# A two-layer diffusion backbone with mixture-of-experts layers: tokens turned inside the gate/up passes, bf16 slot tables, a two-pair weight ring

## The reference

```python
scores = sigmoid(t @ router_w)
sel = scores + router_bias             # 4 of 8 groups, then the top 8 experts of a token
w = take(scores, idx); w = w / sum(w) * ROUTED_SCALE
...                                    # the tokens of each expert, in blocks
yb = (silu(t[tok] @ w_gate[e]) * (t[tok] @ w_up[e])) @ w_down[e] * w_b
routed = zeros.at[tok].add(yb);  out = routed + swiglu(t, shared weights)
```

## Time and profile before

| | |
|---|---|
| median of 3 runs | 2326.23 us (2323.54 to 2328.62) |
| profiled execution | 2326.45 us, its span 2324.6 us |
| TensorE busy | 1915.4 us (82% of the span) |
| VectorE / ScalarE / GpSimd busy | 1145.3 / 794.1 / 318.6 us |
| moved by DMA | 597.07 MB, mean 257 GB/s |
| first expert stage | about 467 to 1208 us |
| second expert stage | about 1702 to 2279 us |

### The profile page before, as it was taken

How to read it: one execution, slowest core, us unless ns; L and a number is a source line. 1 busy time by engine, 2 the same in 40 slices (tenths; PEclk the granted TensorE clock), 3 DMA queues, 4 the chain that set the end, 5 groups by cost and what they waited for, 6 DMA issues and landing times. The chain is left out here.

```text
span 2324.6 us, 33561 instructions
## 1 busy us (share of the span) xinstructions
PE 1915.4 (82%) x9971; PEld 1298.1 (56%) x9972; DVE 1145.3 (49%) x2242; ACT 794.1 (34%) x1292; POOL 318.6 (14%) x333
## 2 busy tenths in 40 slices
PE   2889897899999999999974987637778788878783
PEld 0778744467777777777741971103445555555551
DVE  2325622577777777777748565893131121212114
ACT  1214411155555555555521557870101111111110
POOL 0220010111111211211210101221001111111110
PEclk8999987899999999999987997768889999999997
DMA  6850055068998899999955416304439999999994
GB/s 239 296 188 1 1 224 202 9 251 323 339 339 330 327 342 345 348 333 343 330 191 220 137 55 194 109 18 128 185 144 418 414 392 388 400 411 402 418 366 173
DMA packets 139045, 597.07 MB, mean 257 GB/s; under 512 B 32632, under 2 KB 51128, under 8 KB 79728
## 3 DMA queue, kind: packets, MB, share of 16 engines
q1 hardware_dynamic: 103264, 509.97, 58.3%
q0 software_dynamic: 35584, 84.31, 9.7%
q10 hardware_dynamic: 144, 2.10, 0.2%
HBM read 596.17 MB, written 56.20 MB: 281 GB/s over the span
## 5 line engine op out<-in xcount | busy, mean ns | idle before, releaser
L1459 DVE TENSOR_TENSOR m_w_lo<-m_wgu,m_w_hi 128x1024 fp32r<-128x1024 f32 x264 | 312.6, 1221 | 170.6 <-ACT m_w_hi L1383 157.1
L1383 ACT ACTIVATE m_w_hi<-m_wgu 128x1024 fp32r<-128x1024 f32 x264 | 266.9, 1051 | 205.6 <-DMA m_wgu<-in_moe_w_up 153.0
L1630 PE MATMUL ps<-m_wgu,m_xT 128*64 128x256 f32 x2112 | 261.4, 403 | 78.9 <-DMA m_wgu<-in_moe_w_up 60.1
L1630 PEld LDWEIGHTS ps<-m_wgu,m_xT 128*64 128x64 f32 x2112 | 185.7, 145 | 165.8 <-issue 122.5
L1325 PE MATMUL ps<-m_wd,m_hidT 128*128 128x512 f32 x528 | 237.6, 593 | 0.3 <-ACT m_hidT L1407 0.3
L1340 PE MATMUL ps<-m_w_hi,m_x_hi 128*128 128x512 f32 x528 | 212.8, 403 | 7.2 <-DVE m_x_lo L1451 6.5
L1340 PE MATMUL ps<-m_w_lo,m_x_hi 128*128 128x512 f32 x528 | 208.1, 394 | 0.0
L1340 PE MATMUL ps<-m_w_hi,m_x_lo 128*128 128x512 f32 x528 | 207.2, 392 | 0.0
L1725 DVE SCALAR_TENSOR_TENSOR m_hid<-m_act_g,m_meta,ps 128x256 f32<-128x256 f32 x33 | 15.9, 480 | 337.9 <-ACT m_act_g L1679 337.9
L1325 PEld LDWEIGHTS ps<-m_wd,m_hidT 128*128 128x128 f32 x528 | 95.3, 190 | 95.1 <-issue 95.1
L1266 POOL DMA_INDIRECT y_rows<-h,m_sidx x66 | 67.5, 1023 | 554.5 <-DVE h L1467 554.5
(11 more groups left out here) (316 smaller groups left out, 3429.9 us busy)
## 6 DMA issues: line engine op xcount, KB each, us to landing
m_wgu<-in_moe_w_gate SPq DMA_DIRECT2D x132, 1024.0 KB
m_wgu<-in_moe_w_up SPq DMA_DIRECT2D x132, 1024.0 KB
m_wd<-in_moe_w_down SPq DMA_DIRECT2D x132, 1024.0 KB, 9.9
c_rows<-y_rows SPq DMA_DIRECT2D x12, 2048.0 KB, 15.9
mods<-in_ada_w POOLq DMA_DIRECT2D x11, 1024.0 KB, 6.3
mods<-in_ada_w SPq DMA_DIRECT2D x11, 1024.0 KB, 4.8
mods<-in_lru_w_in SPq DMA_DIRECT2D x7, 1280.0 KB, 6.9
ada_w<-in_ada_w SPq DMA_DIRECT2D x8, 1024.0 KB, 17.5
```

The lines of the kernel that those rows point to most:

```text
L1383: act.activation(w_hi[:, :, k, :], wgu[:, q, :, k, :], ACT.Copy).then_inc(hi_s, 1)
L1459: dve.tensor_tensor(w_lo[:, :, k, :], wgu[:, q, :, k, :], w_hi[:, :, k, :].bitcast(F32), ALU.subtract).then_inc(lo_s, 1)
L1630: last = pe.matmul(g.ps[half[s], GU, a * FE:(a + 1) * FE], xT[:, k, half[s]], wgu[:, s, a, k, :], start=(k == 0), stop=(k == KD - 1))
```

## The change

- First stage, TensorE: `turn_tokens` of the next block stands behind chunk 1 of gate/up (`TURN_AT = 1`) instead of behind chunk 3. ScalarE and VectorE take `tokens` behind their chunk 1, and chunk 2 after it.
- Both stages: `routes.entry` and the one-hot matrices are bf16. Each of the three numbers is stored as three bf16 pieces that add up to it, so the product has 9 columns instead of 3, and VectorE adds the pieces (`tensor_reduce`), then makes the row index from the sum, with a wait between. `pick` is one `scalar_tensor_tensor` for all tiles (one for each block of the pair in the second stage) instead of one `tensor_scalar` for each tile. `route_phase` fills the pieces: some constant fills ahead of the scores, and two subtractions and three copies behind them; a chain of small instructions for each tile goes.
- Second stage: `wgu` holds two pairs, with semaphores for each. `prefetch` issues both pairs (10 MB instead of 6). In the loop the weights of gate and up are loaded two pairs ahead, those of down one pair ahead as before. The loops are unrolled by two; 33 pairs remain.

```diff
-        self.entry = sb(n + "entry", [P, tiles, EXPERTS, 3])
+        self.entry = sb(n + "entry", [P, tiles, EXPERTS, 3 * PIECES], BF16)
...
-        self.wgu = sb(tag + "wgu", [P, 2, 2, KD, FE])
+        self.wgu = sb(tag + "wgu", [P, 2, 2, 2, KD, FE])
...
     def prefetch(self, sp):
...
+        for q in range(2):
+            for s in range(2):
+                self.gate(sp, 2 * q + s, q, s)
+            for s in range(2):
+                self.up(sp, 2 * q + s, q, s)
+            if q == 0:
+                for s in range(2):
+                    self.down(sp, s, s)
...
+                chain.link(dve.tensor_tensor(weight[:], weight[:], wsum[:, :, None].to_broadcast([P, tiles, E]), ALU.mult))
+                for m in range(PIECES):
+                    piece = routes.entry[:, :, :, GAIN * PIECES + m]
+                    chain.link(dve.tensor_copy(piece, weight[:]))
+                    if m + 1 < PIECES:
+                        chain.link(dve.tensor_tensor(weight[:], weight[:], piece, ALU.subtract))
...
-        onehot = sb("onehot", [P, 2, tiles, S])
+        onehot = sb("onehot", [P, 2, tiles, S], BF16)
...
-                        last = pe.matmul(g.ps[0:S, MB + q, 0:3], onehot[:, q, t, :],
+                        last = pe.matmul(g.ps[0:S, MB + q, 0:3 * PIECES], onehot[:, q, t, :],
...
                         last.then_inc(chunk_used, 1)
-                    turn_tokens(i + q, 1 - q)
+                        if c == TURN_AT:
+                            turn_tokens(i + q, 1 - q)
...
                     if split:
-                        split_high(i + q, 1 - q, range(CHUNKS - 1))
+                        split_high(i + q, 1 - q, range(TURN_AT + 1))
+                    tokens(i + q, 1 - q)
+                    if split:
+                        split_high(i + q, 1 - q, range(TURN_AT + 1, CHUNKS - 1))
                     act.wait_ge(chunk_used, CHUNKS * (b + 1))
...
                         split_high(i + q, 1 - q, range(CHUNKS - 1, CHUNKS))
-                    tokens(i + q, 1 - q)
...
-                    for t in range(tiles):
-                        last = dve.tensor_scalar(onehot[:, q, t, :], g.field("iota")[:, 0:S], routes.slot[:, t, bass.ds(e, 1)],
-                                                 g.table[:, bass.ds(b + FIELD[f"negbase{layer}"][0], 1)], ALU.subtract, ALU.is_equal)
-                    last.then_inc(onehot_s, 1)
+                    dve.scalar_tensor_tensor(onehot[:, q, :, :], routes.slot[:, :, bass.ds(e, 1)].to_broadcast([P, tiles, S]),
...
-                    dve.tensor_copy(meta[:, bass.ds(b, 1), :].rearrange("p o c -> p (o c)"), g.ps[0:S, MB + q, 0:3]).then_inc(meta_v, 1)
-                    dve.tensor_scalar(gidx[q][:], g.ps[0:S, MB + q, 0:1], FAR, None, ALU.add).then_inc(idx_s, 1)
+                    pieces = g.ps[0:S, MB + q, 0:3 * PIECES]
+                    dve.tensor_reduce(meta[:, bass.ds(b, 1), :].rearrange("p o c -> p (o c)"), pieces.rearrange("p (c m) -> p c m", m=PIECES),
+                                      AX.X, ALU.add).then_inc(meta_v, 1)
+                    dve.wait_ge(meta_v, b + 1)
+                    dve.tensor_scalar(gidx[q][:], meta[:, bass.ds(b, 1), 0], FAR, None, ALU.add).then_inc(idx_s, 1)
...
+                def gate_up(before, q):
+                    i = before + 1
...
+                    sp.wait_ge(gate_done, before)
                     sp.sem_inc(issue, 1)
                     for s in range(2):
-                        weights.gate(sp, experts[s], s)
-                    sp.wait_ge(up_done, i)
+                        weights.gate(sp, experts[s], q, s)
+                    sp.wait_ge(up_done, before)
...
+                turns = rounds_after_first(sp)
+                with sp.Fori(0, turns) as m:
+                    gate_up(2 * m + 1, 0)
+                    down(2 * m + 1)
+                    gate_up(2 * m + 2, 1)
+                    down(2 * m + 2)
+                gate_up(2 * turns + 1, 0)
+                down(2 * turns + 1)
+                down(2 * turns + 2)
```

More of the change, by code:

```diff
@@ L70 @@
 FAR = 8192.0
+PIECES = 3
+DEST, GAIN = 1, 2
 def slots_of(tiles):
@@ L930, in prefetch @@
     def prefetch(self, sp):
-        for s in range(2):
-            self.gate(sp, s, s)
-        for s in range(2):
-            self.up(sp, s, s)
-        for s in range(2):
-            self.down(sp, s, s)
+        for q in range(2):
[6 more added lines that the diff above has]
+                    self.down(sp, s, s)
 def route_phase(g, layer, tiles, routes, weights):
@@ L1087, in shared_out @@
                     dve.tensor_tensor(g.x[:, t, :], g.x[:, t, :], gated, ALU.add).then_inc(xadd, 1)
+                tok0 = g.field("tok")[:, 0:1, None].to_broadcast([P, tiles, E])
+                for t in range(tiles):
+                    chain.done(dve.memset(routes.entry[:, t, :, 0], t * P - FAR))
+                    chain.done(dve.memset(routes.entry[:, t, :, DEST * PIECES], TOPK * t * P - FAR))
+                chain.done(dve.memset(routes.entry[:, :, :, 2], 0.0))
+                chain.done(dve.tensor_copy(routes.entry[:, :, :, 1], tok0))
+                chain.done(dve.tensor_scalar(routes.entry[:, :, :, DEST * PIECES + 1], tok0, float(TOPK), None, ALU.mult))
                 dve.wait_ge(scored, 1)
@@ L1471, in step @@
                     if split:
-                        split_low(i + q, 1 - q, range(CHUNKS - 1))
+                        split_low(i + q, 1 - q, range(TURN_AT + 1))
+                    tokens(i + q, 1 - q)
+                    if split:
+                        split_low(i + q, 1 - q, range(TURN_AT + 1, CHUNKS - 1))
                     first = isinstance(i, int) and i == 0 and q == 0
@@ L1551, in _, with down @@
             def _(sp):
[L1552 to L1553 removed]
+                def gate_up(before, q):
+                    i = before + 1
                     experts = [owner(sp, 2 * i + s) for s in range(2)]
[L1555 removed]
+                    sp.wait_ge(gate_done, before)
                     sp.sem_inc(issue, 1)
                     for s in range(2):
[L1558 to L1559 removed]
+                        weights.gate(sp, experts[s], q, s)
+                    sp.wait_ge(up_done, before)
                     sp.sem_inc(issue, 1)
                     for s in range(2):
[L1562 removed]
+                        weights.up(sp, experts[s], q, s)
+                def down(i):
+                    experts = [owner(sp, 2 * i + s) for s in range(2)]
                     sp.wait_ge(y_done, i)
@@ L1592, in _ @@
                 scatter(0)
-                with pool.Fori(1, final + 1) as i:
-                    gather(i + 2)
-                    scatter(i)
-                pool.wait_ge(scattered, 16 * final + 16)
+                with pool.Fori(0, turns) as m:
+                    gather(2 * m + 3)
+                    scatter(2 * m + 1)
+                    gather(2 * m + 4)
+                    scatter(2 * m + 2)
+                pool.wait_ge(scattered, 32 * turns + 16)
                 pool.sem_inc(issue, 1)
-                pool.wait_ge(gathered, 16 * final + 48)
+                pool.wait_ge(gathered, 32 * turns + 48)
                 pool.sem_inc(issue, 1)
@@ L1623, in turn_tokens, with project @@
                     last.then_inc(xT_turned, 1)
-                def project(i, a, loaded, done):
-                    pe.wait_ge(loaded, 32 * i + 32)
+                def project(q, r, a, loaded, done):
+                    pe.wait_ge(loaded[q], 32 * r + 32)
                     pe.sem_inc(issue, 1)
@@ L1629, in project, with step @@
                         for s in range(2):
-                            last = pe.matmul(g.ps[half[s], GU, a * FE:(a + 1) * FE], xT[:, k, half[s]], wgu[:, s, a, k, :],
+                            last = pe.matmul(g.ps[half[s], GU, a * FE:(a + 1) * FE], xT[:, k, half[s]], wgu[:, q, s, a, k, :],
                                              start=(k == 0), stop=(k == KD - 1))
                     last.then_inc(done, 1)
-                def step(i):
+                def step(i, q, r):
                     pe.wait_ge(xT_a, i + 1)
@@ L1663, in _ @@
                 turn_tokens(0)
-                final = last_pair(pe)
-                step(0)
-                with pe.Fori(1, final + 1) as i:
-                    step(i)
+                turns = rounds(pe)
+                step(0, 0, 0)
+                with pe.Fori(0, turns) as m:
+                    step(2 * m + 1, 1, m)
+                    step(2 * m + 2, 0, m + 1)
             @block.scalar
@@ L1688, in _ @@
                 tokens(0)
-                final = last_pair(act)
+                turns = rounds(act)
                 step(0)
-                with act.Fori(1, final + 1) as i:
-                    step(i)
+                with act.Fori(0, turns) as m:
+                    step(2 * m + 1)
+                    step(2 * m + 2)
             @block.vector
@@ L1740, in _ @@
                 tokens(0)
-                final = last_pair(dve)
+                turns = rounds(dve)
```

(5 more changed lines are left out.)

68 lines of the change are left out of this document (34 added, 34 removed).

## The result

The changed kernel takes 2329.55 us (median of 20 runs, 2325.62 to 2337.15), the kernel before 2325.90 us beside it (20 runs, 2320.68 to 2328.62). The ratio is 1.0022, with a 95% interval of 1.0014 to 1.0029. So it is slower by 3.7 us (0.2%) where the forecast was 30 us faster, and the time lies 5.6 us above the range. By the prediction's own measure (4.7 us) this is the outcome "within 0.2%", to which it gave 0.08. The profiled span is 2329.3 us against 2324.6.

The account below looks back on a forecast made before the run. TensorE was taken to bound the first expert stage, the DMA engines the second. From 2326.45 us, less 6 (first stage), 4 (starts) and 20 (second stage), came 2296 us; own range 2280 to 2312, wider range 2256 to 2324.

Parts of the forecast that it names:

- within 0.2%: Whole kernel: outcome that the time differs from the kernel before by no more than 4.7 us; chance 0.08.
- The bound: First expert stage limited by TensorE, second by the DMA engines; first-stage weights arrive nearly as late as they may.
- Slots: First stage: four bf16 passes take 0.15 us instead of 0.95; TensorE's own step falls by 0.8 us to 10.15.
- The rival by which they cost as much as before: The bf16 slots save nothing, loads hiding nearly all of it: about 2300 us, chance 0.05.
- The turn: First stage: moved turn asks for rows and weights sooner; 0.7 us stall, step 10.85 against 10.95, 6 us gained.
- The rival with the mid-pass wait: First stage: turn waits for a gather landing at 11.5 us or more; step 11.55, 2340 us; chance 0.12.
- Pick, indices, starts: Both stages: shorter pick and indices, worth nothing in the loop; stages start 1.5 to 3 us sooner, 4 us in all.
- Routing: Routing phases: five chained instructions take a time similar to the replaced per-tile chain; nothing counted, 2 us either way.
- The ring: Second stage: two-pair gate/up buffer prefetches 4.2 MB and raises the rate to 415 GB/s; 20 us counted.
- only the prefetched pair: Second stage: 401 GB/s is what memory gives; 5 us instead of 20, about 2311 us, chance 0.17.
- The gathers behind the deep ring: Second stage: gathers queue behind the backlog and land at about 20 us; about 2400 us, chance 0.03.
- TensorE alone decides: First stage: loads land early enough, step 10.15 to 10.3 us, 41 to 50 us gained, about 2256 us; chance 0.13.

Follow-up runs that it names:

- before_gate_first: The kernel before with only SyncE's first-stage order turned round, gate and up loads ahead of the down load: 2324.11 us, ratio 0.9992 to the kernel before.
- after_gate_first: The changed kernel, early turn kept, with SyncE's first-stage gate and up loads ahead of the down load: 2311.03 us, ratio 0.9935 to the kernel before.
- gather_ahead: The changed kernel with first-stage slots and indices made earlier and the gather issued ahead of the scatter: 2299.10 us, ratio 0.9867 to the kernel before.
- gate_first: The changed kernel with turn and token splits put back late, and first-stage gate and up loads ahead of the down load: 2278.20 us.
- ahead_first: The changed kernel with slots, indices and gather earlier, and first-stage gate and up loads ahead of the down load: 2276.92 us.
- pe_turn: The changed kernel with TensorE's early turn kept, but ScalarE's and VectorE's token splits back at their old places: 2339.50 us, ratio 1.0052 to the kernel before.
- no_turn: The changed kernel with the turn and the token splits back at their old places: 2311.61 us, ratio 0.9931 to the kernel before.

## Why the prediction was wrong, point by point

Forecast 2296, measured 2329.55: 33.5 us apart. By landmarks, the second stage makes 16 of it, the first stage's loop 12, the routing phases 4; the rest lies in code that is the same. Two steps of the prediction failed: the rate of the second stage with the ring, and the size of the turn's stall.

- **The bound.** Right: TensorE in the first stage, the DMA engines in the second, and weights that arrive nearly as late as they may. before_gate_first shows the first of these at its plainest.
- **Slots.** Nearly right in TensorE: 0.31 us for four passes instead of eight (forecast 0.15, within 0.2), and a step of its own of 10.22 to 10.24 us (forecast 10.15). What the saving is worth depends on the loads, as was said. With the late turn and the old order it is 0.15 of 0.7 us. The rival by which they cost as much as before is out, as TensorE's own step did get shorter.
- **The turn: a step that failed, 12 us.** The mechanism (the turn asks for the gathered rows sooner, and the weights' issue hangs on `y_done`) was right, and the trace showed the idle time ahead of the turn that was announced. Two terms were off. I set the gather's landing at 9.6 us, by the scatter's median, and let the two stalls overlap to 0.7 us on a step of 10.15, 10.85 in all. In the stalled steps the gathers took 11.0 us (762.49 to 773.49 above) and 11.3 (after_gate_first) from the end of their issue to the turn; 36 of 63 steps have no stall at the turn, the others up to 2.4 us, and the mean is 11.05. 63 x 0.2 us are 13 us. The second term is the place at which the hidden rows are needed: I took 9.6 us into the step, where their transposes stand, and left out what the sequencer does behind that wait. Measured, the next step starts 2.1 or 2.5 us behind the hidden rows at the earliest, so in a step of 10.2 us they are needed at 8.1 or 7.7. The way to them was right (6.2 us from the weights, forecast 6.3). That the sum came out near even so is partly luck: by it ScalarE would have started on the weights 3.9 us into the step (3.0 + 1.6 - 0.65), and it started at 2.5 on average, from 1.7 to 4.5. The rival with the mid-pass wait named this mechanism at a landing of 11.5 us, but gave it 0.12 since the scatters' highest was 10.4. The turn's own stall is made by the late gathers, and I had used a median where only the tail counts. The deeper fault: I treated the new order as given and asked only what it costs. That the gather goes out behind the step's start although its buffer would be free sooner could be read from the earlier trace rows; gather_ahead and gate_first show what the two orders were worth.
- **Pick, indices, starts.** Right: no cost in the loop, and each stage started 2.0 to 2.2 us sooner, 4 us in all.
- **Routing.** Forecast 0, with 2 us either way; measured 2.0 and 2.2 us in the two phases, 4 in all. I had called the five chained instructions as long as the chain that they replace. VectorE's timeline after has them at 3.6 us from the first cast to the last:

```profile
433.45 0.73 DVE L1150 CAST l_entry<-r_weight 128x256 bf16<-128x256 f32 x1
434.21 0.63 DVE L1152 TENSOR_TENSOR r_weight<-r_weight,l_entry 128x256 f32<-128x256 f32 x1
434.88 0.73 DVE L1150 CAST l_entry<-r_weight 128x256 bf16<-128x256 f32 x1
435.64 0.62 DVE L1152 TENSOR_TENSOR r_weight<-r_weight,l_entry 128x256 f32<-128x256 f32 x1
436.29 0.74 DVE L1150 CAST l_entry<-r_weight 128x256 bf16<-128x256 f32 x1
```

  The removed chain was 1.6 us. This is read from the traces; no kernel undid it alone.
- **The ring: the other step that failed, and the larger.** Forecast 20 us, measured 4.0 (3.6 alone): 16 us, and the rival "only the prefetched pair" (5 us, chance 0.17). The wait did move to the down weights and the gap at the end is there (12 us at a share of 0.24), both as said. What was wrong was the term of 415 GB/s: I read pair windows of 369 and 420 GB/s as a dry and a full queue. With the queue filled well ahead the same spread is there (378 and 424 above), and its mean is 405 to 407. A stretch at 0.99 share has no idle transfers to win; I had read that number and still argued past it. By the Trainium skill's page "DMA: Bandwidth & Descriptors" (the table at its head) the fabric's ceiling is 435 GB/s, and 358 is a core's share of the memory. The sustained 405 of this stage, on one busy core, lie above the second figure and are 93% of the first.
- **The gathers behind the deep ring.** That rival did not come: TensorE's waits of the second stage hold no gather, though some turns come 9.3 us behind the end of the gather's issue, where the rival had the rows land at 20. What they hold (1745 to 2255 us):

```profile
PE ps L1699 <- DMA m_wd<-in_moe_w_down: 89.8, 31, 5.0
PE ps L1688 <- DVE m_hid L1772: 7.8, 31, 0.3
```

  The Trainium skill's rule that an engine goes round between its queues ("DMA: Bandwidth & Descriptors", section "Queues, rings and completion order") agrees with that. It doesn't mean that a gather lands soon: 11.3 us in the first stage.
- **TensorE alone decides.** As a forecast of this kernel wrong, as a bound right: with the loads in time the step is 10.22 to 10.24 us, and gate_first and ahead_first lie at 2278 and 2277, near that rival's 2256 plus the 16 us that the ring did not give.

What stays open is how much of the step each of the sequencer's instructions costs, which DMA engine or packet makes single gathers land at 11 us and others in time, why pe_turn lies 10 us over the changed kernel with steps as long, and whether the second stage's end (a last down load that is issued only when the pair before is done) can be drawn in. Two pairs of down weights were not tried.

## What to carry to other kernels

When a change shortens the engine that is the bound, or asks for data earlier in the step, look at when each load is issued and what stands ahead of it in its queue; the data needed soonest has to go first, and a producer moved forward needs its whole feeding chain (indices, gather, queue place) moved with it. Price a wait by the late tail of the landings, not by their median, since an early arrival gives nothing back. And count what the sequencer does behind a wait (register loads, branches): the operand is needed that much earlier than the matmul that uses it. And where a stretch already shows a DMA share of 1.0, take its mean rate as what there is.

## What the runs showed of the hardware beyond the forecast

- Another order of the same loads in SyncE's program, with no byte and no instruction less, moved a stage from 341 to 359 GB/s and its DMA share from 0.91 to 0.93 over the same 610 us (no_turn and gate_first), and took every wait for weights away. At a share of 0.9 the loads were not short of bandwidth, but of lead: 3 us of earlier issue and 1 MB less ahead of them, which were not tried apart.
- Between a late wait of TensorE's and its next step lay 2.5 us (2.1 where no loop branch follows), though the matmuls in between are done sooner: a register load of 0.30 us and a branch of 0.21 us are among what its sequencer does there. With the slots and their register load moved ahead of the wait it was 1.03 us (gather_ahead).
- A gather of 128 rows issued beside a backlog of large loads took 12.3 us from the start of its issue to its use (820.57 to 832.88), where one with little else running took 4.6.
- VectorE's two-tensor subtraction with a bf16 operand of 256 elements, and the cast into strided bf16 places, took 0.63 and 0.73 us, where the float32 product of the same shape just ahead of them (L1147) took 0.42.
